# Output norm of the recurrent mixer per token tile inside the recurrence's loops, gates earlier, output product as filler of the fifth loop

## What is computed

```python
p = xn @ w_in                                  # 3*512 conv columns, then 3*512 + 288 recurrence columns
y_a = gC * causal_conv(gB * hA)                # 512 features
r, k, v, wd, ad, gd = split(p[..., 1536:])     # after a token shift
g = sigmoid(gd) @ g2                           # gates, rank 160
y = wkv7(r, decay, k, v, kk, a)                # state recurrence over tokens, 8 heads of 64
yn = (y - mean(y)) * rsqrt(var(y) + eps)       # per token and head
y_b = (yn * lnx_w + lnx_b + bonus) * g
out = concat([y_a, y_b]) @ w_out               # 1024 x 1024
h = x + rms_norm(out) * post_mix_g             # then rms_norm(h) * pre_ffn_g @ w_up
```

## Time and profile before

| | |
|---|---|
| median of 3 runs | 1982.78 us (1978.1 to 1984.07) |
| profiled execution | 1974.88 us |
| its span | 1972.8 us |
| PE busy | 1906.2 us, 97% |
| DVE busy | 1145.5 us, 58% |
| ACT busy | 746.7 us, 38% |
| POOL busy | 56.6 us, 3% |
| mean granted TensorE clock | 0.991 of full speed |

### The profile page before, as it was taken

How to read it: one execution, slowest core, us unless ns; L and a number is a source line. 1 busy time by engine, 2 the same in 40 slices (tenths; PEclk the granted TensorE clock), 3 DMA queues, 4 the chain that set the end, 5 groups by cost and what they waited for, 6 DMA issues and landing times.

```text
span 1972.8 us, 30211 instructions
## 1 busy us (share of the span) xinstructions
PE 1906.2 (97%) x12641; PEld 1537.5 (78%) x12641; DVE 1145.5 (58%) x1689; ACT 746.7 (38%) x1070; POOL 56.6 (3%) x77
## 2 busy tenths in 40 slices
PE   6989998899999999999999999999999999999999
PEld 4767775888888888787777778888878777778887
DVE  3574345477676336546677865545445768775544
ACT  4532332422222225533345334333543344434422
POOL 3000000211000000000000000000000000000000
PEclk9999998999999999999999999999999999999999
DMA  4221003233333232322213222323222222222232
GB/s 138 86 64 46 25 24 114 65 82 90 107 87 107 86 128 57 104 64 86 76 64 97 86 65 65 96 97 107 86 65 86 75 65 86 80 93 74 65 107 85
DMA packets 166034, 161.63 MB, mean 82 GB/s; under 512 B 13892, under 2 KB 150378, under 8 KB 165898
## 3 DMA queue, kind: packets, MB, share of 16 engines
q1 hardware_dynamic: 165200, 159.00, 25.5%
q10 hardware_dynamic: 698, 0.71, 0.1%
HBM read 157.59 MB, written 2.10 MB: 81 GB/s over the span
## 4 chain that ended last, share of the span: by engine, by line
PE 75%; DVE 2%; ACT 1%; issue 0%; ACTq 0%; DVEq 0%
PE psum L580 62%; PE psum L1742 5%; PE psum L2235 2%; PE psum L2212 1%; PE psum L570 1%; PE psum L2192 1%; PE psum L2220 1%; DVE w_lo L388 1%; PE psum L518 1%; ACT w_hi L347 0%; PE psum L527 0%; PE psum L2316 0%; DVE h_lo L452 0%; DVE ffn_normed L465 0%; PE psum L2301 0%; DVE w_lo L369 0%
## 5 line engine op out<-in xcount | busy, mean ns | idle before, releaser
L580 PE MATMUL psum<-h_hi,w_hi 128*128 128x512 f32 (+1 forms) x1592 | 622.9, 391 | 17.3 <-DVE h_lo L452 7.4
L580 PE MATMUL psum<-h_lo,w_hi 128*128 128x512 f32 (+1 forms) x1592 | 606.3, 381 | 0.0
L580 PE MATMUL psum<-h_hi,w_lo 128*128 128x512 f32 (+1 forms) x1592 | 606.2, 381 | 0.0
L388 DVE TENSOR_TENSOR w_lo<-w_raw,w_hi 128x2048 fp32r<-128x2048 f32 (+1 forms) x142 | 295.2, 2079 | 277.8 <-ACT w_hi L347 275.3
L347 ACT ACTIVATE w_hi<-w_raw 128x2048 fp32r<-128x2048 f32 (+2 forms) x152 | 266.9, 1756 | 382.0 <-PE psum L580 311.1
L580 PEld LDWEIGHTS psum<-h_hi,w_hi 128*128 128x128 f32 x1592 | 299.8, 188 | 95.8 <-issue 15.0
L580 PEld LDWEIGHTS psum<-h_hi,w_lo 128*128 128x128 f32 x1592 | 300.1, 188 | 58.1
L580 PEld LDWEIGHTS psum<-h_lo,w_hi 128*128 128x128 f32 x1592 | 300.3, 189 | 53.5
L580 PE MATMUL psum<-w_hi,h_hi 128*128 128x512 f32 (+1 forms) x512 | 183.6, 359 | 3.0 <-DVE h_lo L1640 1.9
L580 PE MATMUL psum<-w_lo,h_hi 128*128 128x512 f32 (+1 forms) x512 | 180.3, 352 | 0.0
L580 PE MATMUL psum<-w_hi,h_lo 128*128 128x512 f32 (+1 forms) x512 | 180.1, 352 | 0.0
(11 more groups left out here) (343 smaller groups left out, 2148.3 us busy)
## 6 DMA issues: line engine op xcount, KB each, us to landing
w_raw<-in_w_in_dram SPq DMA_DIRECT2D x170, 512.0 KB, 4.4
w_raw<-in_w_up_dram SPq DMA_DIRECT2D x44, 512.0 KB, 4.8
w_raw<-in_w_out_dram SPq DMA_DIRECT2D x24, 512.0 KB, 4.6
w_raw<-in_w_br_dram SPq DMA_DIRECT2D x48, 256.0 KB, 3.0
w_raw<-in_w_down_dram SPq DMA_DIRECT2D x22, 512.0 KB, 4.3
x_first<-in_x_dram SPq DMA_DIRECT2D x4, 512.0 KB, 5.4
x_tokens<-in_x_dram SPq DMA_DIRECT2D x4, 512.0 KB, 6.3
out_dram<-x_tokens SPq DMA_DIRECT2D x4, 512.0 KB, 2.6
```

The costliest lines, as they stand in the source:

```text
L388: eng.eng.tensor_tensor(m.wl[:, g % 2, 0:n], m.raw[:, g % 2, 0:n], m.wh[:, g % 2, 0:n].bitcast(F32), ALU.subtract).then_inc(eng.done, 1)
L580: last = pe.eng.matmul(out, a(k), b(k), start=(opens and k == 0 and i == 0), stop=(k == kt - 1 and i == 2), skip_group_check=ks is not None)
```

## The change

1. **Gates earlier.** The eight gate matmuls go from behind the fifth loop to behind panel 5. ACT copies them to SBUF (`gates`, four copies, behind `shifted(5)`); in the first loop DVE folds the bias, bonus and gate into `bonus_v`; in the second loop ACT builds a table `y_row_spreads` and scales the gates.
2. **Filler in four loops.** The 80 k-steps go into loops 0 to 3, 20 each.
3. **Norm per token tile.** Tiles 0, 1 and 2 are normed inside loops 2, 3 and 4, tile 3 after them. Each tile: sum, centring, squares, sums, root, reciprocal, spread (eight matmuls of 128 columns), scaling and adding.
4. **Output product as filler.** In the fifth loop, levels 2 to 5, PE does 24 of its 128 steps (one step: three matmuls of 256 columns); levels 0 and 1 have no filler. The rest follows behind the loop, whole tiles first to last.
5. **Splits.** POOL's five `split_lo` go to DVE; the split of panel 15 stands in the fifth loop. x is loaded again behind panel 17, once tile 3 is normed.
6. **Seam.** Its steps run in pairs of tiles; both transposes of the first pair stand before the last output tile.

```diff
 def filler(first, tiles):
-    steps = {}
-    for c in range(TT + 1):
-        steps[c] = 2 if c == 0 else 3
+    slots = {}
+    for c in range(TT):
+        slots[c] = 2
         for l in range(LEVELS):
-            steps[c, l, 0] = 1 if 0 < c < TT else 2
-            steps[c, l, 1] = 1 if c < TT else 0
+            slots[c, l, 0], slots[c, l, 1] = 2, 1
     done, n = {}, 0
-    for slot, k in steps.items():
+    for slot, k in slots.items():
         done[slot] = [(first + i // (2 * KT), i // KT % 2, i % KT) for i in range(n, n + k)]
         n += k
     assert n == tiles * KT
     return done
+
+def y_schedule(first):
+    per = 2 + 3 * LEVELS
+    at = {}
+    for c, offsets in ((2, (2, 5, 6, 8, 11)), (3, (6, 9, 10, 13, 16))):
+        for what, o in zip(("mean", "sums", "root", "split", "spread"), offsets):
+            n = per * c + o
+            at[first + n // (2 * KT), n // KT % 2, n % KT] = (what, c - 2)
+    return at
...
             E.moved(("w raw", p), f"w_loaded{p % 2}", 2)
-            if p == NPROJ + 1:
-                E.wait_ge(dve_done, E.at(("y", 2 * TT - 1)))
+            if p == NP - 1:
+                E.wait_ge(dve_done, E.at(("mix", TT - 1)))
...
     def gpsimd(E):
         constants(E, m)
-        for p in range(NPROJ + 1, NP):
-            split_lo(E, m, p, KT * panels[p][2])
...
+        def gates(j0):
+            for j in (j0, j0 + 1):
+                b = m.bank[E.key(("gate", j))] = aux_bank(("gate out", j))
+                pe.matmul(PS[:, b, :], m.g2a[:, P * j:P * j + P], m.gd[:, :], start=True, stop=False)
+            for j in (j0, j0 + 1):
+                b = m.bank[E.key(("gate", j))]
+                pe.matmul(PS[:, b, :], m.g2b[:, P * j:P * j + P], m.gd2[:, :], start=False,
+                          stop=True).then_inc(pe_done, 1)
+                E.counted(("gate", j))
 
...
         panel(4, only=1)
         panel(5)
+        E.wait_ge(*E.point("g2 loaded"))
+        gates(0)
+        gates(2)
         E.wait_ge(dve_done, E.at("rn"))
         E.wait_ge(act_done, E.at(("ind", 1)))
         spread = []
...
+        def y_mean(t, b):
+            E.wait_ge(dve_done, E.at(("y", 2 * t + 1)))
+            banks.use(b, ("y centred", t))
+            m.bank[E.key(("y mean", t))] = b
+            pe.matmul(PS[:, b, :], m.bd[:, :], m.yT[:, :, P * t:P * t + P], start=True, stop=True).then_inc(pe_done, 1)
+            E.counted(("y mean", t))
+
...
+        def y_spread(t, b):
+            E.wait_ge(dve_done, E.at(("y rstd", t)))
+            E.wait_ge(act_done, E.at(("spread rows", JT - 1)))
+            banks.use(b, ("y scaled", t))
+            m.bank[E.key(("y rstd spread", t))] = b
+            for j in range(JT):
+                o = PS[:, b, P * j:P * j + P]
+                pe.matmul(o, m.spreadY[:, j, :], m.rnH[:, 0:P], start=True, stop=False)
+                last = pe.matmul(o, m.spreadY[:, j, :], m.rnL[:, 0:P], start=False, stop=True)
+            last.then_inc(pe_done, 1)
+            E.counted(("y rstd spread", t))
+
...
+        def out_step(i, t, k):
+            if k == 0:
+                E.wait_ge(*E.point(("w lo", NPROJ + i)))
+                E.wait_ge(dve_done, E.at(("mix lo", 0, t // 2)))
+                if i == 0:
+                    banks.use(2 * t, seam.key("post out", t))
+            if k == JT:
+                E.wait_ge(dve_done, E.at(("mix lo", 1, t)))
+            last = out_part(i, t, [k])
+            if k == KT - 1:
+                last.then_inc(pe_done, 1)
+                E.counted(("out mm", i, t))
+                if t == TT - 1:
+                    E.alias(("w used", NPROJ + i), ("out mm", i, t))
+
+        early = [(i, t, k) for i, t in ((0, 0), (1, 0), (0, 1)) for k in range(KT)]
+
+        def last_fill(l):
+            n = len(early) // (LEVELS - 2)
+            for i, t, k in early[n * (l - 2):n * (l - 1)] if l > 1 else ():
+                out_step(i, t, k)
...
+            if c == TT:
+                y_mean(TT - 2, 1)
...
                 fill((c, l, 0))
+                if c == TT:
+                    last_fill(l)
+                    if l == 1:
+                        y_sums(TT - 2, 3)
+                    if l == 3:
+                        y_spread(TT - 2, 1)
...
-        E.wait_ge(dve_done, E.at(("mix lo", KT - 1)))
+        y_mean(TT - 1, 7)
+        for k in range(KT):
+            out_step(1, 1, k)
+        y_sums(TT - 1, 5)
+        for k in range(KT):
+            out_step(0, 2, k)
+        y_spread(TT - 1, 7)
+        for k in range(KT):
+            out_step(1, 2, k)
         for i in range(2):
-            for t in range(TT):
-                out_part(i, t, range(JT, KT)).then_inc(pe_done, 1)
-                E.counted(("out mm", i, t))
-            E.alias(("w used", NPROJ + i), ("out mm", i, TT - 1))
-        for i, t in ((2, 0), (2, 1), (3, 0), (2, 2), (3, 1), (2, 3), (3, 2), (3, 3)):
+            for k in range(KT):
+                out_step(i, 3, k)
+        for i, t in ((2, 0), (2, 1), (3, 0), (3, 1), (2, 2), (2, 3), (3, 2), (3, 3)):
             E.wait_ge(*E.point(("w lo", NPROJ + i)))
             if i == 2:
                 banks.use(2 * t + 1, seam.key("post out", t))
...
-            if i == 3 and t >= 2:
-                seam_turn(E, m, banks, seam, t - 2)
+            if (i, t) == (3, 2):
+                seam_turn(E, m, banks, seam, 0)
+                seam_turn(E, m, banks, seam, 1)
...
         decays(3)
         shifted(5)
+        def gates(j0):
+            for j in (j0, j0 + 1):
+                E.wait_ge(act_done, E.so_far())
+                E.wait_ge(pe_done, E.at(("gate", j)))
+                act.activation(m.gate[:, j, :], PS[:, m.bank[E.key(("gate", j))], :], ACT.Copy).then_inc(act_done, 1)
+                E.counted(("gate out", j))
+
+        gates(0)
+        gates(2)
         shifted(6)
         shifted(7)
...
+        def gates_scaled():
+            E.wait_ge(act_done, E.so_far())
+            E.wait_ge(pe_done, E.at(("rn spread", JT - 1)))
+            act.activation(m.spreadY[:, :, :].rearrange("p j n -> p (j n)"), m.rnH[:, :].bitcast(F32), ACT.Copy,
+                           scale=0.0).then_inc(act_done, 1)
+            E.counted("spread rows zero")
+            E.wait_ge(act_done, E.so_far())
+            for j in range(JT):
+                q = slice(RS * j, RS * j + RS)
+                act.activation(m.spreadY[q, j, :], m.indT[q, HALF_Q, :].bitcast(F32), ACT.Copy).then_inc(act_done, 1)
+                E.counted(("spread rows", j))
+            for j in range(JT):
+                E.wait_ge(dve_done, E.at(("bonus gated", j)))
+                act.activation(m.gate[:, j, :], m.gate[:, j, :], ACT.Copy, scale=col("lnx_w", j)).then_inc(act_done, 1)
+                E.counted(("gate scaled", j))
...
+                if c == 1 and l == 0:
+                    gates_scaled()
+                if c == TT:
+                    if l == 0:
+                        mix_hi(0, 0, 0, 2)
+                    if l == 1:
+                        mix_hi(1, 1, 0, 2)
+                        y_root(TT - 2)
+                    if l == 2:
+                        split(NPROJ + 1)
+                    if l == 3:
+                        mix_hi(0, 1, 2, 4)
+                    if l == 4:
+                        mix_hi(1, 2, 2, 3)
...
+        y_square(TT - 1)
+        y_root(TT - 1)
+        mix_hi(1, 3, 3, 4)
+        split_hi_halves(E, m, 16, KT * PW)
...
+        def y_mixed(t):
+            E.wait_ge(dve_done, E.so_far())
+            E.wait_ge(pe_done, E.at(("y rstd spread", t)))
+            dve.tensor_tensor(y_tile(t), by_tile("y rstd spread", t), y_tile(t), ALU.mult).then_inc(dve_done, 1)
+            E.counted(("y scaled", t))
+            E.wait_ge(dve_done, E.so_far())
+            dve.tensor_tensor(y_tile(t), y_tile(t), m.bv[:, :, P * t:P * t + P], ALU.add).then_inc(dve_done, 1)
+            E.counted(("mix", t))
+
...
+                if c == 0 and l < JT:
+                    bonus_gated(l)
+                if c == TT:
+                    if l == 0:
+                        mix_lo(0, 0, 0, 2, (0,))
+                    if l == 1:
+                        mix_lo(1, 1, 0, 2, (0, 1))
+                        y_weighed(TT - 2)
+                        y_var(TT - 2)
+                    if l == 2:
+                        y_rstd(TT - 2)
+                        split(NPROJ + 1)
+                    if l == 3:
+                        y_mixed(TT - 2)
+                    if l == 4:
+                        mix_lo(0, 1, 2, 4, (1,))
+                        mix_lo(1, 2, 2, 3, (2,))
...
+        y_centred(TT - 1)
+        y_weighed(TT - 1)
+        y_var(TT - 1)
+        y_rstd(TT - 1)
+        y_mixed(TT - 1)
+        mix_lo(1, 3, 3, 4, (3,))
+        split_lo_halves(E, m, NPROJ + 2, KT * PW)
+        split(NPROJ + 3)
...
         pool = E.eng
-        for p in range(2):
-            split_lo(E, m, base + p, PANEL)
...
     def vector(E):
         dve = E.eng
-        post_add(E, m, seam, 0)
```

(19 more changed lines are left out.)

254 lines of the change are left out of this document (128 added, 126 removed).

## The result

The changed kernel takes **1960.65 us** (median of 4, 1960.0 to 1962.4); the kernel before, now with four executions, 1980.8 (1978.1 to 1984.1). The ratio is 0.989, with a 95% interval from 0.987 to 0.992.

The account below looks back on a forecast made before the run. PE was taken as the bound, busy 97% of the span, with gains only where it idles or runs at the lower clock. +9.2 + 8.9 + 4.9 + 5.6 - 39.4 = -10.8 us, applied to the 1982.8 median: 1972.0 us, range 1962 to 1982.

Parts of the forecast that it names:

- A: Before the loops: gates behind panel 5 take 8.3 us, PE waits 5.6, two waits (4.7) vanish; loops start 9.2 later.
- B: Loops 1 to 4: loops 2 to 4 take 20 k-steps instead of 15, 10.4 us more, 1.5 recovered: +8.9 us.
- C: Norm of tiles 0 and 1 inside loops 3 and 4: 4.4 us, plus 0.5 for DVE pieces ahead of an inverse: +4.9.
- T0: Start of the fifth loop, 284.2 us in the profile before; the third feed-forward panel started 138.8 us later.
- D: From the fifth loop's start to the third feed-forward panel: 99.4 us instead of 138.8, so 39.4 us less.
- E: Lower clock behind long new waits only: 3.8 us behind the gates and 1.8 from T0 onwards, together +5.6 us.
- rival 5: Loops 1 to 4: added DVE and ACT steps lengthen the recurrence's chain by 18.8 us; +8.0, 1990.8 us; chance 0.06.
- 1: Rival, loops 1 to 4: the added k-steps fall into waits and the clock holds; -18.4, 1964.4 us; chance 0.20.
- 2: Rival, gates behind panel 5: no stall there and no clock loss from it; -20.2, 1962.6 us; chance 0.06.
- 3: Rival, fifth loop: the output product is no filler, 8.6 us lost; -2.2, 1980.6 us; chance 0.08.
- 4: Rival, gates, bare levels, split and seam: clock falls at every new wait, 15.2 us not 5.6; -1.2, 1981.6; chance 0.10.

Follow-up runs that it names:

- the two edits: Changed kernel with ACT's gate copies earlier (1956.1 us) or the key-norm spread between panel 6's halves (1954.9 us); both, with two early splits, 1949.0 us.
- the zeros: Kernel before with matmuls of zeros, which change nothing, put on PE into five of its waits: 1982.0 us with long groups, 1976.3 us with short ones.
- no_filler: Changed kernel with the 24 early output-product steps moved from the fifth loop to right behind its last matmul: 1970.0 us.
- before_busy: Kernel before with groups of 16, 18, 10, 28 and 14 zero matmuls put on PE into five waits: 1982.0 us, ratio 1.000.

## Why the prediction was right and wrong

The working, against the profiled execution it was made for:

| step | predicted us | profile after |
|---|---|---|
| start of the loops (A, and the clock behind the gates) | +13.0 | +13.0, of which 1.6 arose ahead of the gates |
| the four loops (B and C) | +13.8 | +10.5 |
| T0 to the third panel (D, and 1.8 of clock) | -37.6 | -37.7 |
| sum at the third panel | -10.8 | -14.2 |
| behind it | 0 | +2.0 |

- **A** was right in kind and nearly in size: gates 7.6 us instead of 8.3, stall 6.6 instead of 5.6, both waits behind it gone (4.7). With 2.5 of clock (see E) and the 1.6 that arose ahead of the gates this makes 13.6; what the other -0.6 is stays open. That the row agrees to 0.1 us is luck: the 1.6 us are chance, in the second profile of the changed kernel the gates start at 97.35. The stall was avoidable: the two edits together removed it.
- **B and C**: loops 3 and 4 grew by 5.5 and 5.3 us, as 5 k-steps (3.4) and one tile of the norm (2.2) say. I had taken 1.5 us as recovered; none was there. Loop 1, which my sum left alone, grew by 1.6 us: PE waits 1.48 and 0.85 us in it where it had waited 0.69, and DVE's four new `bonus_v` steps (0.75 us each) stand ahead of steps of the inverse. That is rival 5's mechanism, in small. But loop 2 got 1.9 us shorter: in the profile of before it held a pause of 2.06 us in PE's issue (1.96 and 1.79 in the other two profiles, none after) and a half-rate stretch from 196 to 203 us, neither of which I had read.
- **D** was right within 1.7 us, wait by wait: at the split of level 3 1.82 (predicted 1.5), at panel 16 0.92 (0.6), at the seam 1.88 and 2.50 (1.9, 2.5).
- **E** had the place behind the gates right and the size wrong: 2.5 us instead of 3.8. From the spread's first matmul to the eleventh of panel 6 PE takes 5.56 us (113.35 to 118.91), before the change 3.07 (97.56 to 100.63). The mean of 0.79 counts also the half rate of 109 to 113.3 us, while PE stood idle, which costs nothing. The 3.8 came from the earlier trace rows and was too much there as well: of the half rate between 336 and 353 us only 1.5 us were paid, the rest was hidden ahead of a wait (see the zeros). The 1.8 behind T0 did not come. That only long waits lower the clock is refuted: `no_filler` had a clock of 0.57 over 20 us with no wait over 2.73, and waits of 1.85 and 2.50 us went with 0.72 over 6 us.
- **Behind the third panel** the 2.0 us are mostly clock too: 1.5 arise behind the wait of 2.50 us in the second layer, where only the first profile of the kernel before kept full clock.
- **The step that failed** is the last: "It lies 0.4% below the median of the three runs, so I apply the difference to the median". I took that distance as something the change leaves alone. It is mostly time at the lower clock. Between the first and the second profile of the kernel before lie 6.6 us: 1.2 ahead of the spread, 1.2 in loop 2, -1.5 in the fifth loop, 4.1 behind the wait for `x_tile` and 1.5 in the second layer. In the loops and at the seam, where the change fills or removes PE's waits, both profiles of the changed kernel have full clock; at the start and in the second layer they run the same risk as before. So a usual execution has more to win than the one I had read. (1 - clock) x span is 17.8 us for the profiled execution before and 21.8 for a usual one (1979.8 at 0.989), and 11.8 for one at 0.994 after. So up to about 10 of the 20 us are clock, an upper bound, since half rate while PE is idle or ahead of a wait costs nothing. Second profiles of both kernels differ by 21.6 us (1981.52 and 1959.94), and 21.5 of them are there at the third panel (428.05 and 406.56). Of the 11.3 us between forecast and result, 7.9 are this step (1982.8 - 1974.88; 2.0 of them because the median of three executions lay that much above that of four), 1.7 the sum's own error (10.8 against 12.5) and 1.7 the distance of the changed kernel's profiled execution from its median.
- **Rivals**: 1 (the clock holds) comes nearest, though its k-steps did not fall into waits; its time of 1964.4 shares the wrong base. 2, 3 and 5 are out as wholes. 4 is refuted for the changed kernel, but its mechanism is that of `no_filler`.

What stays open: why a given wait lowers the clock in one execution and not in the next, and what the pause in PE's issue in loop 2 was.

## What to carry to other kernels

Before a difference is applied to a median, ask what separates the profiled execution from the usual ones: with a span and a mean clock for each, (1 - clock) x span says how much of the spread can be clock, and a change that fills PE's short waits can remove that as well. Half rate counts only where PE is the bound: ahead of a wait that another engine ends it costs nothing, so compare the starts of the same matmuls and not the windows' mean clock alone. Filler inside a dependent chain is worth more than the waits it covers (9 us for 24 steps here, of which 3.6 by waits). A moved step that holds PSUM banks needs its reader moved along on the other engine, or independent matmuls put before the next user of the banks.

## What the runs showed of the hardware

- One program's time varied by 17 us over 81 executions, and followed its mean granted clock with 2.1 us per 0.001; half-rate stretches came and went at the same places and behind the same waits.
- Half rate ahead of a wait was hidden by it: the transposes of `x_tile` started 9.87, 9.88 and 9.89 us after the same earlier matmul, with half rate between them only in the first profile.
- While PE stood idle for 6.58 us before the spread, the granted clock fell to 0.50; it was 0.50 also for the work from 113.3 to 118.7 us.
- A DVE add of two SBUF tensors waits out a whole POOL split (1.23 us becomes 4.99); one with a PSUM input is not touched (0.69).
- A float32 matmul of 64 x 64 by 128 columns stood as two instructions and took 0.23 us (32 instructions in 3.66 us in `before_busy`), twice the 0.11 that I had assumed; eight transposes of 128 columns took 1.09.
